# Reordering the sums of 512 slots on TensorE, and moving four weight loads on GpSimd's queue

## The chip, the core and the metric

The kernel runs on one core of one Trainium2 chip. The metric is the device time of one execution in microseconds. Before the change it is 2069.1 us, the median of three runs (2067.74 to 2071.44). Besides these runs there is one execution taken by the hardware profiler, and all rows below come from it.

## The reference, cut to what matters

Two transformer blocks over 256 tokens of width 1024, all in float32. The first block (recurrence, sparse attention, feed-forward) lies ahead of everything that the change touches. The second block has two layers; each ends in a layer of experts:

```python
s = einsum('thpe,pne->thpn', q, sub_keys)          # 8 heads, 2 halves, 128 keys
top_s, top_i = top_k(s, 16)
cand = top_s[:, :, 0, :, None] + top_s[:, :, 1, None, :]
best_s, best_j = top_k(cand, 16)                    # 16 experts a head of 16384
gate = softmax(best_s)
h = einsum('td,thkd->thk', x, u[expert])            # 128 experts a token
a = gelu(h) * gate
f = einsum('thk,thkd->td', a, v[expert])
```

Every token has experts of its own, so each row of `u` and `v` (1024 numbers each) has to be fetched from memory by index. The first layer mixes tokens by gated linear attention, the second by dilated attention with six heads of three groups. Both also attend to a memory of 256 tokens.

## The kernel before

Tokens lie on the 128 partitions, in two tiles. A pass is one layer of experts for one tile; there are four, in the order (layer 0, tile 0), (0, 1), (1, 0), (1, 1). A pass has 128 slots: slot s takes the s-th expert of each of its 128 tokens. All in all n runs from 0 to 511 (`SLOTS`). For each slot

- GpSimd issues one indirect DMA (L2254) that gathers 128 rows of u and v, 1 MB, into one of six buffers (`gbuf`, `GBUF = 6`); from n = 6 on it waits for `buffer_free` of slot n - 6, that is for the end of that slot's sum;
- VectorE multiplies the u half by x and adds up along the row, the dot (L2544), once the gather has landed;
- ScalarE takes the Gelu of the dot (L2082) and makes a diagonal matrix of gate x gelu (L2076, L2089; five buffers, `DIAGS`);
- TensorE multiplies that diagonal by the v half, two products of 512 columns that add into two PSUM banks over the whole pass (`add_slot`, L1456). That is the sum of the slot; it waits for `diag_ready`.

Beside the gathers of pass p, TensorE makes what is next: in pass 0 the queries and keys of the first layer of experts, in passes 1 and 2 the whole second layer for tiles 0 and 1: transposes, the products of dilated attention and of memory attention, the output product, the queries and keys of the experts; the last of these reach into the next pass. `pe_steps()` is a table written out by hand that says at which slot each of these products stands; `act_steps()` and `dve_steps()` say at which slot ScalarE and VectorE take their results, for most of them three slots later (`LATER = 3`). Each engine works through its table in order. ScalarE and VectorE do a slot's table entries before that slot's own diagonal or dot; VectorE's include the routing (top-k) of later experts and the soft-max of the scores. All of these products run through the helper at L925, so that rows of TensorE name L925 for them and L1456 for the sums. A product that streams its weights takes them from a ring of eight slots, filled in pairs of 1 MB by SyncE's queue (L1677).

The second layer's expert queries need 16 blocks of weights of 512 KB for each tile. The eight even ones (`KEPT`) are loaded once and kept in SBUF for both tiles, by `load_kept(i)` on GpSimd's queue. Blocks 0 to 3 have a place of their own and are loaded early. Blocks 4 to 7 go where the first layer's linear attention had its operands: 4 to 6 are loaded behind the wait for `gla_intra` (L2221), in front of the eighth row of gains and the weights of the first heads (`head_w`, L2231); 7 is loaded when the third sum of the linear attention is filled (`gla_o`, L2237). TensorE first waits for the kept blocks, all eight of them, at slot 224.

Of the kernel before, what the change touches and what calls it, by code (L numbers as in the profile page):

```python
# [17 lines left out]
P = 128  # L18
# [7 lines left out]
KEPT = tuple(range(0, 16, 2))  # L26
# [15 lines left out]
GBUF = 6  # L42
# [585 lines left out]
def build(nc, x_in, memT_in, weights, consts, where, rows_in, peer_uv, out):  # L628
# [5 lines left out]
    with ctx:  # L634
# [5 lines left out]
        def sem(name):  # L640

            if name not in named:
                named[name] = ctx.enter_context(nc.semaphore(name))
            return named[name]
# [190 lines left out]
        def wait_filled(e, key):  # L835

            e.wait_ge(sem("psum_filled"), ids[key] + 1)

        def wait_drained(e, key):

            n = ids[key]
            e.wait_ge(sem("drained_by_" + drains[n]), freed_count[n])

        def bank(key):
            return ps[banks[ids[key]]]
# [23 lines left out]
        def load_row(e, n):  # L869

            e.dma_start(rows[:, n % NROW, :], rows_in[n:n + 1, :].to_broadcast([P, D]))\  # L871
                .then_inc(sem(row_sem(n)), 16)
# [5 lines left out]
        def slot_of(q):  # L878

            return PASSES[q // P] + (q % P,)  # L880

        def wait_freed(e, q):

            e.wait_ge(sem(f"buffer_free{q % GBUF}"), q // GBUF + 1)
# [14 lines left out]
        def _(pe):  # L899
# [32 lines left out]
            def begin(key):  # L932

                b = before[ids[key]]
                if b is not None:
                    pe.wait_ge(sem("drained_by_" + drains[b]), freed_count[b])
                return bank(key)
# [512 lines left out]
            def add_slot(n):  # L1450

                pe.wait_ge(sem("diag_ready"), n + 1)
                for h in range(2):
                    key = (f"sum{n // P}", h)
                    b = begin(key) if n % P == 0 else bank(key)
                    ins = pe.matmul(b[:, :], diag[n % DIAGS], gbuf[n % GBUF][:, 1, h * 512:(h + 1) * 512],  # L1456
                                    start=n % P == 0, stop=n % P == P - 1)
                    if n == SLOTS - 1:
                        ins.then_inc(sem("psum_filled"), 1)
                    elif h == 1:  # L1460
                        ins.then_inc(sem(f"buffer_free{n % GBUF}"), 1)
                if n == SLOTS - P + CARRY:
                    pe.wait_ge(sem("alpha_ready"), 1)
                    for h in range(2):
                        pe.matmul(bank((f"sum{n // P}", h))[:, :], alpha_diag, x[:, NT - 1, h * 512:(h + 1) * 512],
                                  start=False, stop=False)
                if n % P == P - 1 and n < SLOTS - 1:

                    wait_freed(pe, n)
                    pe.sem_inc(sem("psum_filled"), 2)  # L1470
# [98 lines left out]
            def peer_keys(o, g):  # L1569

                wait_drained(pe, (f"peer_q1_{o}_{g}", 0))
                b = begin((f"peer_s1_{o}_{g}", 0))
                for hp in range(2 * TH):
                    mm(b[:, hp * P:(hp + 1) * P], tile_pq(g)[:, hp, :], c("keysT", 2, 2, PN)[:, 1, hp % 2, :],
                       True, True, end=hp == 2 * TH - 1)

            for n in range(SLOTS):
                for name, what in PE_STEPS.get(n, []):
                    if name == "second_turn":
                        pe.wait_ge(sem("x_ready"), 6)  # L1580
# [12 lines left out]
                    if name == "mem_k":  # L1593
                        i, half = what
# [5 lines left out]
                    if name == "mem_v" and n < P:  # L1600
                        i, half = what
# [17 lines left out]
                    if name == "dil_k":  # L1619
                        o, i = what  # L1620
# [5 lines left out]
                    if name == "qm":  # L1626
                        o, i = what
# [28 lines left out]
                    if name == "peer_q":  # L1656
                        o, g, i = what
# [5 lines left out]
                        block_of((f"peer_q1_{o}_{g}", 0), i, 4, tile_xT, kept=kept)  # L1663
                    if name == "peer_s":
                        peer_keys(*what)
                add_slot(n)

        @block.sync
        def _(sp):
# [517 lines left out]
        @block.gpsimd  # L2187
        def _(pool):

            pool.wait_ge(sem("psum_filled"), ids[("xT_mix", 3)] + 1)  # L2190
            pool.dma_start(cst[:, n_early:], consts[:, n_early:n_const]).then_inc(sem("consts_loaded"), 16)
            pool.wait_ge(sem("lru_scanned"), 1)
            pool.wait_ge(sem("gr_shaped"), 1)
            for j in range(NK):
                pool.tensor_tensor(xc[:, j, :], xc[:, j, :], gr[:, j, :], ALU.mult).then_inc(sem("pool_step"), 1)
            for j in range(NK + 1):
                if j < NK:
                    pool.wait_ge(sem("pool_step"), j + 1)
                    pool.wait_ge(sem("gmr_shaped"), j + 1)
                    pool.tensor_tensor(gmr[:, j, :], gmr[:, j, :], xc[:, j, :], ALU.mult).then_inc(sem("pool_step"), 1)  # L2200
                if j:
                    pool.wait_ge(sem("pool_step"), NK + j)
                    pool.tensor_tensor(xc[:, j - 1, :], xc[:, j - 1, :], gmr[:, j - 1, :], ALU.add)\
                        .then_inc(sem("recurrence_gated"), 1)
            pool.wait_ge(sem("psum_filled"), ids[("att_gate", 2 * len(GATES) - 1)] + 1)
            for n in range(NROW):
                load_row(pool, n)

            def load_kept(i):

                pool.dma_start(kept_queries[i], weights[n_slots - 8 + i // 2, :, i % 2 * SLOT:(i % 2 + 1) * SLOT])\
                    .then_inc(sem("kept_queries_loaded"), 16)

            for i in range(4):
                load_kept(i)
            pool.wait_ge(sem("psum_filled"), ids[("att_turn", 2 * len(UNITS) - 1)] + 1)
            pool.dma_start(memT[:, :, :], memT_in.rearrange("(k p) s -> p k s", p=P)).then_inc(sem("memT_loaded"), 16)
            pool.dma_start(spread, consts[:, n_const:]).then_inc(sem("spread_loaded"), 16)
            for r in range(NROW, SPREAD):
                if r == NROW + 3:  # L2220
                    wait_drained(pool, ("gla_intra", 0))  # L2221
                    pool.dma_start(kept_w, weights[n_slots - 2, :, :]).then_inc(sem("kept_loaded"), 16)
                    for i in range(4, len(KEPT) - 1):
                        load_kept(i)
                pool.wait_ge(sem("rows_used"), r - NROW + 1)
                load_row(pool, r)
                if r == 7:
                    wait_filled(pool, ("gla_r", 3))
                    wait_drained(pool, ("mem_value0", 2 * len(MEM_UNITS) - 2))
                    for i in range(4):  # L2230
                        pool.dma_start(head_w[i], weights[n_slots - 4 + i // 2, :, i % 2 * SLOT:(i % 2 + 1) * SLOT])\  # L2231
                            .then_inc(sem("head_loaded"), 16)
                    last = weights[n_slots - 1, :, :]
                    pool.dma_start(area(25168, 1024), last[:, 0:1024]).then_inc(sem("kept_out_loaded"), 16)
                    for i, m in enumerate((mem_k, mem_v)):
                        pool.dma_start(kept_out[1][i], last[:, 1024 + 512 * i:1536 + 512 * i]).then_inc(sem("kept_out_loaded"), 16)
            wait_filled(pool, ("gla_o", 3))  # L2237
            load_kept(len(KEPT) - 1)
            for n in range(SLOTS):
                l, t, s = slot_of(n)  # L2240
                if n == 0:
                    pool.wait_ge(sem("first_expert"), 1)
                elif n == 1:
                    pool.wait_ge(sem("next_experts"), 1)
                elif n == PK // 2:
                    pool.wait_ge(sem("peer_experts"), ROUTE_NO[0, 0, 0])
                elif (l, t, s) in ROUTE_NO:
                    pool.wait_ge(sem("peer_experts"), ROUTE_NO[l, t, s])
                if n == MIX_BUF:
                    wait_filled(pool, ("out0_1", 1))  # L2250
                if n >= GBUF:
                    wait_freed(pool, n - GBUF)
                pool.sem_inc(sem("gather_turn"), 1)
                pool.indirect_dma_start(gbuf[n % GBUF].rearrange("p a d -> p (a d)"), None, peer_uv,  # L2254
                                        bass.IndirectOffsetOnAxis(ap=expert[t][:, s:s + 1].bitcast(U32), axis=0))\
                    .then_inc(sem(f"gathered{n % GBUF}"), 16)
# [840 lines left out]
```

## Time and profile before

| | us |
|---|---|
| median of three runs | 2069.1 |
| profiled execution | 2072.7 |
| its span, first to last instruction | 2070.9 |
| TensorE busy with matmuls | 1895.9 |
| VectorE busy | 1382.5 |
| ScalarE busy | 896.6 |
| GpSimd busy | 616.1 |
| first gather issued at | 627.0 |

A page of the profile gives for each engine its busy time, and the span in 40 equal slices (51.8 us each) with the rate that the DMA engines moved. A row of the order of time has the start in us from the span's start, the duration, engine, line, operation, tiles, the number of records, and in brackets how long the engine was idle before it and what ended that. TensorE's matmuls are pipelined and their ends are modelled, so that the last record of a group reaches a little over the start of the next.

### The profile page before, as it was taken

The page shows a single profiled execution, that of the slowest core. Times are in us where ns is not written, and L with a number is a line of the kernel's source. Part 1 is how long each engine was busy: PE and PEld are TensorE (multiplying, and loading weights), DVE is VectorE, ACT ScalarE, POOL GpSimd, SP SyncE. Part 2 cuts the span into 40 slices and gives each one's busy share as a digit, 9 for nine tenths or more (in the row PEclk, how much of TensorE's full clock was granted, in tenths as well). Part 3 has the DMA queues.
Part 4 walks back from the last instruction along what each step waited for, and adds up shares of the span by engine and source line. Part 5 has one row for each costly group of instructions (what it writes and reads, how often), then busy time and mean ns, then how long its engine had stood idle before and what let it go on. Part 6 is the DMA issues. An engine that isn't in the chain of part 4 may idle for free. (4 is left out here: it accounts for less than half of the span.)

```text
span 2070.9 us, 24820 instructions
## 1 busy us (share of the span) xinstructions
PE 1895.9 (92%) x8012; PEld 1169.3 (56%) x8012; DVE 1382.5 (67%) x2957; ACT 896.6 (43%) x2417; POOL 616.1 (30%) x567
## 2 busy tenths in 40 slices
PE   8999999999998999988899998999999899877776
PEld 8788668887955654433456544556664355322222
DVE  8778666666738677776665545766865575985444
ACT  5657454444534333333334533343455334343332
POOL 0002200000003344444333334443334434444442
PEclk9999999999999999999999999999999999999999
DMA  6623555554658999999999999999999999999997
GB/s 253 224 108 123 194 184 192 193 183 152 235 186 354 390 421 419 418 418 414 400 421 421 421 419 410 417 422 421 417 414 391 416 416 387 422 421 419 421 419 317
DMA packets 99373, 708.06 MB, mean 342 GB/s; under 512 B 11040, under 2 KB 11184, under 8 KB 14896
## 3 DMA queue, kind: packets, MB, share of 16 engines
q0 software_dynamic: 77504, 552.25, 65.1%
q1 hardware_dynamic: 21600, 154.15, 19.8%
q8 instruction: 64, 1.05, 0.2%
q14 instruction: 61, 0.50, 0.1%
q10 hardware_dynamic: 144, 0.11, 0.0%
HBM read 705.42 MB, written 1.05 MB: 341 GB/s over the span
## 5 line engine op out<-in xcount | busy, mean ns | idle before, releaser
L1456 PE MATMUL bank<-arena 128*128 128x512 f32 x2048 | 980.6, 609 | 145.4 <-ACT arena L2089 142.1
L2544 DVE SCALAR_TENSOR_TENSOR arena<-arena,x_tok 128x1024 f32<-128x1024 f32 x512 | 627.1, 1226 | 466.7 <-DMA arena<-peer_uv,arena 461.1
L2254 POOL DMA_INDIRECT arena<-peer_uv,arena x512 | 580.9, 1135 | 850.1 <-PE bank L1456 649.4
L1456 PEld LDWEIGHTS bank<-arena 128*128 128x128 f32 x2048 | 362.0, 191 | 639.4 <-ACT arena L2089 339.7
L2082 ACT ACTIVATE arena<-arena 128x1 f32<-128x1 f32 x512 | 103.6, 202 | 841.7 <-DVE arena L2544 837.7
L2089 ACT ACTIVATE arena<-arena 128x128 f32<-128x128 f32 x512 | 197.7, 386 | 0.5
L2076 ACT ACTIVATE arena<-const_tile,arena 128x128 f32<-128x128 f32 x512 | 197.8, 386 | 0.0
L925 PEld LDWEIGHTS bank<-xT,weight_ring 128*128 128x128 f32 x1248 | 165.5, 191 | 37.0 <-issue 31.1
L925 PE MATMUL bank<-xT,weight_ring 128*128 128x128 f32 (+1 forms) x1248 | 177.2, 294 | 0.9 <-DVE xT L2281 0.9
L925 PE MATMUL bank<-x_low_high,z_high 128*128 128x512 f32 (+1 forms) x480 | 135.8, 351 | 1.5 <-issue 1.5
L1201 PE MATMUL bank<-x_split,w_split 128*128 128x512 f32 x704 | 129.0, 342 | 2.6 <-DVE x_split L2824 2.6
L1201 PEld LDWEIGHTS bank<-x_split,w_split 128*128 128x128 f32 x704 | 110.4, 190 | 20.0 <-issue 2.8
L2806 DVE TENSOR_TENSOR w_split<-weight_ring,w_split 128x1024 fp32r<-128x1024 f32 x66 | 80.8, 1225 | 36.9 <-ACT w_split L1917 36.2
L925 PE MATMUL bank<-x_low_high,ring_low 128*128 128x256 f32 x368 | 104.0, 283 | 0.0
L925 PEld LDWEIGHTS bank<-x_low_high,z_high 128*128 128x128 f32 x480 | 83.5, 190 | 17.1 <-issue 5.2
L871 POOL DMA_DIRECT2D row_ring<-rows_in x8 | 4.5, 571 | 286.6 <-DVEq L2354 200.4
L1917 ACT ACTIVATE w_split<-weight_ring 128x1024 fp32r<-128x1024 f32 x66 | 69.7, 1060 | 42.7 <-PE bank L1201 26.6
L1704 ACT ACTIVATE arena<-bank 128x512 f32<-128x512 f32 (+6 forms) x143 | 67.7, 498 | 45.0 <-PE bank L925 38.1
L925 PE MATMUL bank<-arena 128*64 128x128 f32 (+10 forms) x664 | 74.7, 311 | 2.5 <-DVE arena L2304 1.8
L925 PEld LDWEIGHTS bank<-x_low_high,ring_low 128*128 128x128 f32 x368 | 70.5, 192 | 0.0
L925 PEld LDWEIGHTS bank<-arena 64*128 64x128 f32 (+6 forms) x664 | 54.4, 169 | 28.1 <-issue 23.6
L1767 ACT ACTIVATE z_high<-weight_ring 128x1024 fp32r<-128x1024 f32 x50 | 51.8, 1053 | 34.3 <-PE bank L925 25.5
(322 smaller groups left out, 2035.7 us busy)
## 6 DMA issues: line engine op xcount, KB each, us to landing
weight_ring<-weights SPq DMA_DIRECT2D x145, 1024.0 KB
arena<-peer_uv,arena POOLq DMA_INDIRECT x512
arena<-weights POOLq DMA_DIRECT2D x9, 512.0 KB, 7.9
row_ring<-rows_in POOLq DMA_DIRECT2D x8, 512.0 KB, 4.7
kept_queries<-weights POOLq DMA_DIRECT2D x4, 512.0 KB, 9.8
const_tile<-consts POOLq DMA_DIRECT2D x1, 1657.0 KB, 8.9
x_tok<-x_in SPq DMA_DIRECT2D x2, 512.0 KB, 4.9
memT<-memT_in POOLq DMA_DIRECT2D x1, 1024.0 KB, 7.5
```

Of the source, the lines that this page charges most:

```text
L925: ins = pe.matmul(o, lhsT, rhs, start=start, stop=stop, is_transpose=turn or None)
L1201: ins = pe.matmul(o, lhsT, rhs, start=start, stop=stop)
L1456: ins = pe.matmul(b[:, :], diag[n % DIAGS], gbuf[n % GBUF][:, 1, h * 512:(h + 1) * 512], start=n % P == 0, stop=n % P == P - 1)
L1704: done(act.activation(o, i, f, **kw), "drained_by_act" if last else "act_step")
L1767: done(act.activation(z_high[:, i % SPLITS, :], ring[:, slot % RING, :], ACT.Copy, scale=scale), "z_high")
L1917: done(act.activation(w_split[n % SPLITS][:, 0, :], ring[:, slot % RING, :], ACT.Copy), "slot_high")
L2076: done(act.activation(gate_diag[n % 2], ident, ACT.Copy, scale=w[:, s:s + 1]), "gate_diag")
L2082: done(act.activation(hdot[:, s:s + 1], hdot[:, s:s + 1], ACT.Gelu), "peer_gelu")
L2089: done(act.activation(diag[n % DIAGS], gate_diag[n % 2], ACT.Copy, scale=hdot[:, s:s + 1]), "diag_ready")
L2254: pool.indirect_dma_start(gbuf[n % GBUF].rearrange("p a d -> p (a d)"), None, peer_uv, bass.IndirectOffsetOnAxis(ap=expert[t][:, s:s + 1]. ...
L2544: dve.scalar_tensor_tensor(u, u, 1.0, x[:, t, :], ALU.mult, ALU.mult, accum_out=hdot[:, s:s + 1])\
L2806: done(dve.tensor_tensor(w[:, 1, :], ring[:, slot % RING, :], w[:, 0, :], ALU.subtract), name)
```

## The change

Two things. First, in the loop over the slots on TensorE, the sum of slot n is put ahead of the other products of slot n in place of behind them. This holds from slot 12 (two rounds of the six buffers) on, and not for the first and the last slot of a pass. Second, on GpSimd's queue the loads of kept blocks 4 to 6 stand behind the loads of the first heads' weights and of the output weights, and block 7 is loaded at slot 64 of the first pass, between the wait for the buffer and the gather of that slot. The wait for `gla_o` is dropped.

```diff
@@ -1575,6 +1575,9 @@
             for n in range(SLOTS):
+                ahead = 0 < n % P < P - 1 and n >= 2 * GBUF
+                if ahead:
+                    add_slot(n)
                 for name, what in PE_STEPS.get(n, []):
...
@@ -1663,7 +1666,8 @@
                     if name == "peer_s":
                         peer_keys(*what)
-                add_slot(n)
+                if not ahead:
+                    add_slot(n)
...
@@ -2220,8 +2224,6 @@
                     pool.dma_start(kept_w, weights[n_slots - 2, :, :]).then_inc(sem("kept_loaded"), 16)
-                    for i in range(4, len(KEPT) - 1):
-                        load_kept(i)
                 pool.wait_ge(sem("rows_used"), r - NROW + 1)
...
@@ -2234,8 +2236,8 @@
-            wait_filled(pool, ("gla_o", 3))
-            load_kept(len(KEPT) - 1)
+            for i in range(4, min(len(KEPT), 7)):
+                load_kept(i)
             for n in range(SLOTS):
...
@@ -2250,6 +2252,8 @@
                 if n >= GBUF:
                     wait_freed(pool, n - GBUF)
+                if n == 2 * P // 4 and len(KEPT) == 8:
+                    load_kept(7)
                 pool.sem_inc(sem("gather_turn"), 1)
```

## Rows read from the trace of the kernel before

**Rows 1.** The page: the span, and the DMA rate in 40 slices.

```profile
span 2070.9 us, 24820 instructions
...
GB/s 253 224 108 123 194 184 192 193 183 152 235 186 354 390 421 419 418 418 414 400 421 421 421 419 410 417 422 421 417 414 391 416 416 387 422 421 419 421 419 317
```

**Rows 2.** Waits, whole span: who waited for whom, us, times, longest.

```profile
POOL arena L2254 <- PE bank L1456: 649.4, 347, 9.2
...
DVE arena L2544 <- DMA arena<-peer_uv,arena: 461.1, 376, 3.7
```

**Rows 3.** Order of time, a slot with nothing but its gather and sum.

```profile
1906.87 1.98 PE L1456 MATMUL bank<-arena 128*128 128x512 f32 x4 [0.50 <-ACT arena L2089]
...
1907.24 1.23 DVE L2544 SCALAR_TENSOR_TENSOR arena<-arena,x_tok 128x1024 f32<-128x1024 f32 x1 [1.25 <-DMA arena<-peer_uv,arena]
...
1908.91 0.39 ACT L2089 ACTIVATE arena<-arena 128x128 f32<-128x128 f32 x1
...
1909.35 1.12 PE L1456 MATMUL bank<-arena 128*128 128x512 f32 x2 [0.50 <-ACT arena L2089]
...
1909.98 1.79 POOL L2254 DMA_INDIRECT arena<-peer_uv,arena  x1 [1.86 <-issue]
```

**Rows 4.** Busy time by stretch: PE, PEld, DVE, ACT, POOL, granted clock, DMA share, GB/s.

```profile
1560.00:1580.00 20.00, 18.63 (x79) 10.90 (x78) 12.09 (x25) 13.56 (x34) 8.80 (x7) 1.00 0.98 378
...
1700.00:1720.00 20.00, 20.00 (x97) 12.93 (x97) 15.01 (x30) 10.84 (x31) 7.26 (x7) 1.00 0.98 373
```

**Rows 5.** Order of time, TensorE and ScalarE, slots 293 to 295.

```profile
1482.45 3.70 PE L1456 MATMUL bank<-arena 128*128 128x512 f32 x8 [0.93 <-ACT arena L2089]
...
1485.72 0.39 ACT L2089 ACTIVATE arena<-arena 128x128 f32<-128x128 f32 x1
...
1489.07 1.88 PE L1456 MATMUL bank<-arena 128*128 128x512 f32 x4
```

**Rows 6.** Order of time, TensorE and ScalarE, slots 370 to 373.

```profile
1704.78 1.95 PE L925 MATMUL bank<-const_tile,arena 128*128 128x128 f32 x16
...
1706.16 0.39 ACT L2089 ACTIVATE arena<-arena 128x128 f32<-128x128 f32 x1
...
1706.60 1.98 PE L1456 MATMUL bank<-arena 128*128 128x512 f32 x4
...
1710.20 1.88 PE L1456 MATMUL bank<-arena 128*128 128x512 f32 x4
...
1712.81 3.60 PE L1456 MATMUL bank<-arena 128*128 128x512 f32 x8
```

**Rows 7.** Order of time, gather 378 on GpSimd and its dot.

```profile
1715.51 0.94 POOL L2254 DMA_INDIRECT arena<-peer_uv,arena  x1 [1.67 <-PE bank L1456]
...
1723.24 1.22 DVE L2544 SCALAR_TENSOR_TENSOR arena<-arena,x_tok 128x1024 f32<-128x1024 f32 x1 [1.25 <-DMA arena<-peer_uv,arena]
```

**Rows 8.** Order of time: waits for products at slots 64 and 318.

```profile
820.90 0.38 ACT L1704 ACTIVATE arena<-bank 128x256 f32<-128x256 f32 x1 [2.98 <-PE bank L925]
...
1551.86 1.88 PE L1456 MATMUL bank<-arena 128*128 128x512 f32 x4
...
1556.09 3.70 PE L1456 MATMUL bank<-arena 128*128 128x512 f32 x8
...
1556.19 0.76 DVE L2585 COPY arena<-bank 128x256 f32<-128x256 f32 x2 [3.02 <-PE bank L925]
```

**Rows 9.** Order of time on GpSimd: kept loads and the first gather.

```profile
560.07 1.57 POOL L2211 DMA_DIRECT2D arena<-weights  x3
...
619.22 0.54 POOL L2211 DMA_DIRECT2D arena<-weights  x1 [24.52 <-PE bank L925]
626.98 1.02 POOL L2254 DMA_INDIRECT arena<-peer_uv,arena  x1 [7.22 <-DVE arena L2474]
```

**Rows 10.** Busy time by stretch, ahead of the gathers (columns as in Rows 4).

```profile
570.00:580.00 10.00, 9.26 (x65) 7.59 (x64) 8.72 (x18) 5.50 (x15) 0.00 (x0) 1.00 0.57 222
...
600.00:610.00 10.00, 10.00 (x24) 4.18 (x22) 3.14 (x6) 0.29 (x1) 0.00 (x0) 1.00 0.26 105
```

## The prediction

> **What bounds the kernel now.** I read the page first, then the waits, then the DMA rate by stretch, then the order of time in the stretches where that rate falls. From 673 us to the end the DMA engines move about 421 GB/s in most of the page's slices [rows 1]: 512 gathers of 1 MB, one a slot, and the weights between them. In the waits VectorE stands for the landing of gathers and GpSimd for TensorE, whose sum of slot n frees the buffer of gather n + 6 [rows 2]. Where a slot carries nothing else, sums come 2.48 us apart (1906.87 and 1909.35): a dot starts at the landing (1907.24), its diagonal ends at 1909.30, the sum starts at 1909.35, and the gather that a sum lets go is issued 1.1 us behind that sum's end (1908.85, then 1909.98) [rows 3]. So the stage goes at the pace of its DMA bytes. A sum that ends earlier pays only where the DMA has too few gathers before it.
>
> How much that is can be read off one row. The page's slices are 51.8 us wide; each slice's shortfall is (421 - x) / 421 x 51.8 us. From the slice at 673 us on these add up to about 21 us [rows 1]. Slice 390 (3.8 us) is the start of the loop, and its hole lies at 672 to 688 us, before sum 12 can free a buffer. Slice 400 (2.6 us) and slice 410 (1.3 us) lie where a layer norm holds the dots and so the diagonals. What TensorE's order can touch is the slice 391 (3.7 us, 1553 to 1605), 387 (4.2 us, 1708 to 1760), and small ones (two of 414, two of 416 and others, about 5 us together). Inside the two large ones TensorE is busy 18.63 and 20.00 of 20 us and the rate is 378 and 373 GB/s at a DMA share of 0.98 [rows 4]: packets last longer there, they hardly stop.
>
> **Part 1, the order on TensorE.** Call A(n) the sum of slot n (four records, 1.72 us), and W(n) that slot's other products: 16 records, 1.78 us, for a block of 128 columns; 8 records, 0.89 us. Nothing is added or taken away. Before, A(n) can start at the later of its diagonal and the end of W(n); after, at the later of its diagonal and the end of W(n - 1), which stands behind A(n - 1). Two things follow. Where TensorE waits for data at every slot, nothing changes. Where it is behind, A(n) moves by W(n0) - W(n), with n0 the last slot at which it still waited: a block that used to fill the wait for the diagonal of n0 now comes behind A(n0) and is paid in full. So the change can go either way, stretch by stretch. I worked it through the four stretches below; the slots are counted by the sums, four records each (a ninth record or a missing one shows up as x9 or x7).
>
> Gain (slots 295 to 303). TensorE waited 0.93 us before the sum of slot 293, with no product there; sums 293 and 294 follow each other from 1482.45 to 1485.9, and A(295) starts at 1489.07, behind 3.1 us of products, though its diagonal was there at 1486.11 (1485.72 + 0.39) [rows 5]. So W(n0) = 0: sums 295 and 296 come 2.9 us earlier, 297 1.6 us, and so gathers 301 to 303. The slices there are short by 0.4 and 0.9 us, and that is all that can be won. With the other small shortfalls I take -1.5 us for all of these, bounds -3.0 and 0.
>
> Loss (slots 370 to 389). W(370) runs from 1704.78 and ends just as the diagonal of 370 gets ready (1706.16 + 0.39): it was hidden [rows 6]. W(371) lies between 1708.3 and 1710.20, W(372) between 1711.9 and 1712.81. After the change A(370) still starts at 1706.6, then come W(370) to 1710.1, A(371) to 1711.8 (before: 1710.20 to 1711.92, no change), W(371) to 1713.6, and A(372) at 1713.6 in place of 1712.81; W(372) is 0.89, so A(373) starts at 1716.2 in place of 1714.5, and A(374) at 1717.9 (before 1718.03). From there a sum without products of its own (375, 377, 378, 380, 382, and on to 389) is 1.6 to 1.7 us later, and one with a block is where it was. Eleven gathers go out later, in just the stretch in which the DMA is short of them: gather 378 is issued at 1715.51 and its dot starts at 1723.24, 7.7 us later [rows 7], where the full rate goes with 9 to 10 us. Each microsecond of lateness is lost once, as all later landings then shift. Bounds: 0, and 3.4 us (twice the shift, since the rate is low too); I take +1.5.
>
> The scores (slots 309 to 326). VectorE waited 3.02 us at 1556.19 for the products of memory attention that end W(315) (L2585), with the dot of slot 318, whose data had landed, queued behind [rows 8]. A(314) started at 1551.86 and A(315) at 1556.09, so W(315) is 2.5 us; W(313) and W(314) are like W(295), 3.1 each. W(309) holds scores too, and 1.7 us more on them puts the diagonal and sum of slot 313 at about 1546.4. From there three sums and three sets, 3 x 1.72 + 3.1 + 3.1 + 2.5 = 13.9, end these scores at 1560.3 in place of 1556.1, so the dot, ScalarE's diagonal, the sums 317 to 320 and gathers 323 to 326 are 1.5 to 2.7 us late. Against that, gathers 319 and 320 go out up to 3 us earlier. Bounds -2.0 (half of the slice's shortfall won) and +3.5; I take +1.2. The same products stand in pass 1 (slots 184 to 203), with no shortfall now but with sums 188 to 190 up to 2.5 us later: bounds 0 and 1.8, I take +0.8. At slot 64 ScalarE waited 2.98 us for W(63) ahead of that slot's diagonal [rows 8]; W(63) now ends 2.2 us later, and sums 64 to 66 with it, while 62 and 63 come 1.3 us earlier: bounds -0.4 and +1.8, I take +0.2.
>
> **Part 2, the loads of the kept slots.** Three loads of 512 KB leave the POOL queue at 560.07, and follow the loads that end at 594.7 (24.52 us of idle before 619.22) [rows 9]. What they left: TensorE was busy 9.26 of 10 us at 570 to 580, so at most 0.7 us could be won; its one gap there ended with a ScalarE drain that began as the transposes ended, so I take 0. What they enter: 1.5 MB at 421 GB/s is 3.7 us, in 600 to 610, where the DMA moves 105 GB/s at a share of 0.26 [rows 10]; they stand behind the head weights in their queue, so these don't wait. The cover is that empty stretch; without it they would cost 3.7 us. The wait for the third sum of the linear attention goes too, but GpSimd's first gather at 626.98 stood for VectorE's index (7.22 us) anyway: 0. The last load moves from 619.22, where it cost nothing, to slot 64, in front of gather 64: 0.5 MB at 421 GB/s is 1.2 us of the resource that sets the pace, plus 0.54 us of issue on GpSimd, hidden as gathers go out some 10 us ahead of their dots there. Bounds 0 (it falls into a hole made by ScalarE's wait) and 1.2; I take +1.2.
>
> The Trainium skill speaks to this move. DMA: Bandwidth & Descriptors, Rules for kernel authors, says to issue a DMA early and wait for it late; by that rule the load should have stayed at 619, and the sum would be 1.2 us less. Its section Issuing engines are not separate DMA queues says that all DMAs share the same 16 engines, so that a load from another queue would cost the same here. The trace can't show the moved load, but the even 421 GB/s of [rows 1] has no room for it.
>
> **The sum.** +1.2 (load) - 1.5 (heavy slots and small holes) + 1.2 (slice 391) + 1.5 (slice 387) + 0.8 (pass 1) + 0.2 (slot 64) + 0 (front) = +3.4 us. The profiled execution took 2072.7 us (span 2070.9 and 1.8 around it) and would take 2076.1; the runs' median is 2069.1, so I forecast 2072.5 us. All lower bounds together give 2063, all upper ones 2081.
>
> **The rivals.** (1) The order helps as a buffer freed early: the holes of slices 391 and 387 don't deepen, the heavy slots win their 3.0 and the scores 2.0, slot 64 0.4; with the load's 1.2 that is -4.2, 2064.9 us. For it: TensorE is behind its diagonals by 3 us at slot 295 [rows 5]. Against it: the hidden blocks. (2) Clearly slower: the scores behind two sums hold the dots. It decides from the point at which a score ends later than its dot's data lands, in both passes. Price: 3.5 in place of 1.2 and 1.8 in place of 0.8, so +3.4 + 3.3 = +6.7, 2075.8 us. For it: the wait of 3.02 us is there already [rows 8]. Against it: in pass 1 VectorE doesn't wait at all. (3) The reordering does nothing, as the DMA sets the pace and a gather early or late by 2 us is absorbed by the queue; only the load counts: 2070.3 us. A rule of the skill stands for (3): Perfetto Trace Analysis, Identifying the Most-Contended Engine, has one improve the engine with the highest occupancy first, and that is the DMA here.
>
> **How the numbers follow.** The forecast holds 0.35, (1) 0.20, (2) 0.25, (3) 0.20. A measurement of this kernel can tell about 0.2% from no change, that is 4.1 us: under 2065.0 is faster, over 2073.2 slower. (1) lies on the edge, and with the low tail of (3) gives 0.15 for faster; (2) and near a third of the forecast's spread give 0.35 for slower; 0.50 stays for within. The range from 2064.5 to 2078.0 holds the forecast, (3), most of (2) and half of (1).
>
> **What would show it.** In the profile after: the load of 512 KB at slot 64, near 808 us, and a DMA rate not under 420 there; slice 387 lower than 387; VectorE's wait at L2585 near 1556 longer than 3.02 us; the slice at 1501 up from 414; nothing changed before 627 us and after 1770 us but a shift. The forecast is wrong if slices 391 and 387 rise towards 421, or if TensorE's start moves ahead of 627.

## The result, and where the time went

The changed kernel takes 2079.9 us (median of five runs, 2079.0 to 2087.4) beside 2069.1 for the kernel before: a ratio of 1.0053, with a 95% interval from 1.0036 to 1.0069. The medians differ by 10.8 us, where 3.4 were forecast. The forecast of 2072.5 and its range up to 2078.0 were both too low.

The profiled execution of the changed kernel, the page's span and DMA rate in 40 slices (these answer to [rows 1]):

```profile
span 2078.1 us, 24821 instructions
...
GB/s 237 223 137 108 203 196 192 190 162 182 203 183 386 400 418 415 421 416 417 409 421 416 398 413 414 415 422 421 421 394 372 410 418 373 420 422 421 421 421 317
```

A slice is 52.0 us now. Four slices are low that weren't, or weren't as much: 398 (1143 to 1195 us, pass 1), 394 and 372 (1507 to 1611, pass 2; 414 and 391 before), and 373 (1714 to 1766; 387 before). The first gather goes out at 623.27, 3.7 us earlier than at 626.98 [rows 9]. That is not the change: in the twelve kernels below it goes out between 620 and 627, whichever place the loads have. So I count from there. From the first gather to the end of the span it was 1443.9 us before and is 1454.8 after: 10.9 us, as much as the medians differ by.

The surest way to see where they lie is the landing of the gathers (a gather lands where its last packet comes in, and where VectorE waits for it its dot starts there, as in [rows 3]). The time between two landings, in us:

| gathers | before | after | order alone | loads alone | scores ahead | copies later | memory scores ahead |
|---|---|---|---|---|---|---|---|
| 0 to 60 | 175.7 | 176.5 | 176.8 | 176.1 | 175.9 | 176.1 | 175.8 |
| 60 to 130 | 181.7 | 182.7 | 181.8 | 183.0 | 182.7 | 183.5 | 182.9 |
| 130 to 175 | 142.1 | 141.3 | 141.0 | 141.5 | 141.0 | 141.0 | 141.1 |
| 175 to 205 | 84.7 | 89.1 | 89.7 | 84.8 | 85.4 | 85.6 | 86.2 |
| 205 to 290 | 251.3 | 250.3 | 253.6 | 251.3 | 253.3 | 251.2 | 250.8 |
| 290 to 306 | 50.4 | 48.5 | 47.7 | 50.4 | 47.9 | 49.4 | 48.7 |
| 306 to 345 | 116.8 | 124.1 | 123.0 | 116.9 | 117.3 | 118.3 | 118.2 |
| 345 to 395 | 134.0 | 135.1 | 137.6 | 136.2 | 136.1 | 136.9 | 137.5 |
| 395 to 511 | 290.5 | 290.6 | 291.8 | 290.2 | 290.7 | 290.9 | 291.6 |

Each column is one profiled execution; kernels that don't differ in a stretch lie up to 1 to 3.5 us apart there (gathers 205 to 290 take 250.3 to 253.6 us in the five kernels with the new order). The columns from "order alone" on belong to experiments that are told below. Of the 10.9 us, +7.3 lie between gathers 306 and 345 and +4.4 between 175 and 205, the two places where memory scores are taken. Slots 290 to 306 won 1.9. All else adds up to +1.1.

Who waited for whom in the changed kernel, from 661 to 2066 us (us in total, times, longest; [rows 2] is over the whole span):

```profile
POOL arena L2258 <- PE bank L1456: 655.8, 345, 4.9
DVE arena L2548 <- DMA arena<-peer_uv,arena: 436.3, 360, 3.7
...
ACT arena L1708 <- PE bank L925: 31.8, 18, 5.3
DVE arena L2589 <- PE bank L925: 19.1, 4, 6.8
DVE arena L2571 <- PE bank L925: 6.4, 3, 2.7
DVE xT L2605 <- PE bank L925: 6.0, 6, 2.7
```

Lines stand 3 or 4 lower than before: L2589 is VectorE's copy of the memory scores (L2585 before), L2571 that of the dilated scores, L2605 that of the attention values. Before, L2585 waited 4.1 us in two waits (1.12 at 1536.62, and the 3.02 of [rows 8]) and the other two not at all. ScalarE's waits for products (L1708) grew as well, from 10.9 us in four waits over the same stretch to 31.8 in eighteen; the experiments below show that they are not what costs the time. Order of time on VectorE in pass 2 (answers to the last row of [rows 8]):

```profile
1538.12 0.76 DVE L2589 COPY arena<-bank 128x256 f32<-128x256 f32 x2 [4.63 <-PE bank L925]
...
1550.82 1.02 DVE L2571 SCALAR_TENSOR_TENSOR arena<-bank,const_tile 128x512 f32<-128x512 f32 x2 [2.70 <-PE bank L925]
...
1562.01 0.76 DVE L2589 COPY arena<-bank 128x256 f32<-128x256 f32 x2 [6.76 <-PE bank L925]
...
1563.52 1.23 DVE L2548 SCALAR_TENSOR_TENSOR arena<-arena,x_tok 128x1024 f32<-128x1024 f32 x1
```

The dot at 1563.52 is that of slot 318, whose data had landed at 1554.24: 9.3 us behind its data (3.3 before). What TensorE did meanwhile:

```profile
1535.51 1.95 PE L925 MATMUL bank<-xT,weight_ring 128*128 128x128 f32 x16
1537.39 0.70 PE L925 MATMUL bank<-mem_k,arena 64*128 64x256 f32 x4
1538.02 5.71 PE L1456 MATMUL bank<-arena 128*128 128x512 f32 x12
1543.56 0.61 PE L925 MATMUL bank<-arena,memT 128*128 128x128 f32 x4
1546.24 3.65 PE L1456 MATMUL bank<-arena 128*128 128x512 f32 x4 [2.07 <-ACT arena L2093]
1549.68 1.54 PE L925 MATMUL bank<-arena 128*128 128x256 f32 x6
...
1561.28 0.70 PE L925 MATMUL bank<-mem_k,arena 64*128 64x256 f32 x4
```

The rows of 64x256 are the memory scores of slots 309 and 315. Between them TensorE ran out of work for 2.07 us: behind the wait of 4.63 us the dot of slot 313 started at 1541.30, 1.9 us after its data had landed, ScalarE did an exponential before its diagonal (ready at 1546.19), and the blocks that could have filled the wait (L925 at 1549.68 and on) now stand behind that sum. Then the sum itself took 3.65 us for four records in place of 1.88. The stretches (columns as in [rows 4]) say why:

```profile
1544.00:1546.00 2.00, 0.17 (x2) 0.00 (x0) 1.86 (x6) 1.97 (x5) 1.22 (x1) 1.00 1.00 418
1546.00:1550.00 4.00, 3.76 (x6) 1.67 (x7) 1.37 (x3) 1.70 (x7) 0.00 (x0) 0.57 1.01 418
1550.00:1554.00 4.00, 4.00 (x25) 3.28 (x24) 3.11 (x4) 0.00 (x0) 0.94 (x1) 1.00 0.89 311
1554.00:1558.00 4.00, 4.00 (x31) 3.51 (x30) 1.25 (x4) 2.66 (x6) 0.94 (x1) 1.00 0.64 209
```

The granted clock is 0.57 from 1546 to 1550, that is at its lower level (1.2 GHz) for nearly all of the sum, right behind the 2.07 us of idling. And the last two rows show the price: the DMA falls to 311 and 209 GB/s, and its share to 0.64. Over 50 us, first in the kernel before, then in the changed kernel, the rate went from 389 to 343 GB/s and the DMA's share from 0.99 to 0.93:

```profile
1550.00:1600.00 50.00, 47.14 (x190) 26.17 (x189) 28.38 (x55) 26.97 (x74) 21.78 (x19) 1.00 0.99 389
1550.00:1600.00 50.00, 46.24 (x208) 27.97 (x207) 27.33 (x51) 24.91 (x65) 17.82 (x17) 1.00 0.93 343
```

GpSimd issues the gathers 319 to 322 into this hole:

```profile
1550.70 0.94 POOL L2258 DMA_INDIRECT arena<-peer_uv,arena  x1 [4.94 <-PE bank L1456]
1555.52 0.94 POOL L2258 DMA_INDIRECT arena<-peer_uv,arena  x1 [3.89 <-issue]
1560.69 0.94 POOL L2258 DMA_INDIRECT arena<-peer_uv,arena  x1 [4.24 <-issue]
1564.72 0.95 POOL L2258 DMA_INDIRECT arena<-peer_uv,arena  x1 [3.09 <-PE bank L1456]
```

They stand 4 to 5 us apart, where a landing every 2.48 us needs one every 2.48 us. Before, 319 to 321 stood as far apart (1549.71, 1554.86, 1558.89), but 322 followed after 1.7 us, at 1560.60. And one more thing differs: a weight load of 1 MB on SyncE's queue, first in the kernel before, then in the changed kernel.

```profile
1550.64 0.33 SPq L1677 DMA_DIRECT2D weight_ring<-weights  x1
1556.46 0.33 SPq L1681 DMA_DIRECT2D weight_ring<-weights  x1
```

Before, its bytes moved at 1552 to 1558 us, just where only about two gathers were under way, and the rate from 1554 to 1558 us was 395 GB/s. In the changed kernel it goes out 5.8 us later, and its bytes move from 1560 us on, behind the hole. So in these traces late gathers and a late weight load make the hole together; what each is worth alone was not measured. Counted from the landing of gather 306 (1518.4 before, 1517.1 after), gather 320 goes out 2.0 us later than before, 321 3.2, and 322 to 328 between 4.6 and 7.2.

### The profile page after: what moved, and what is told of

It is laid out like the page before. It is cut to its first block and busy times, and to the rows that moved or that the text cites. A ratio compares the mean times of both kernels' runs of the same rounds, so it can differ in the third digit from the quotient of the medians.

```text
span 2078.1 us, 24821 instructions
## 1 busy us (share of the span) xinstructions
PE 1893.3 (91%) x8012; PEld 1166.7 (56%) x8012; DVE 1383.0 (67%) x2957; ACT 897.8 (43%) x2417; POOL 615.1 (30%) x567
## 5 line engine op out<-in xcount | busy, mean ns | idle before, releaser
L925 PEld LDWEIGHTS bank<-xT,weight_ring 128*128 128x128 f32 x1248 | 167.2, 193 | 37.7 <-issue 30.9
L925 PE MATMUL bank<-xT,weight_ring 128*128 128x128 f32 (+1 forms) x1248 | 179.5, 296 | 0.8 <-DVE xT L2285 0.8
L925 PE MATMUL bank<-x_low_high,z_high 128*128 128x512 f32 (+1 forms) x480 | 136.0, 351 | 0.0
L925 PE MATMUL bank<-x_low_high,ring_low 128*128 128x256 f32 x368 | 104.2, 283 | 0.0
L1708 ACT ACTIVATE arena<-bank 128x512 f32<-128x512 f32 (+6 forms) x143 | 68.1, 500 | 71.6 <-PE bank L925 63.4
L925 PEld LDWEIGHTS bank<-x_low_high,z_high 128*128 128x128 f32 x480 | 83.7, 190 | 15.0 <-issue 2.9
L925 PE MATMUL bank<-arena 128*64 128x128 f32 (+10 forms) x664 | 72.9, 305 | 1.8 <-DVE arena L2308 1.0
L925 PEld LDWEIGHTS bank<-x_low_high,ring_low 128*128 128x128 f32 x368 | 70.8, 192 | 0.0
L925 PEld LDWEIGHTS bank<-arena 64*128 64x128 f32 (+6 forms) x664 | 52.7, 161 | 27.8 <-issue 24.0
L925 PE MATMUL bank<-weight_ring,arena 128*128 128x512 f32 (+1 forms) x192 | 64.9, 528 | 0.2 <-ACT arena L1708 0.2
```

What stands on the lines that cost most here:

```text
L925: ins = pe.matmul(o, lhsT, rhs, start=start, stop=stop, is_transpose=turn or None)
L1708: done(act.activation(o, i, f, **kw), "drained_by_act" if last else "act_step")
```

## The experiments

The theory, T: a product that VectorE waits for ends later, the dots behind it in VectorE's queue start late, so diagonals, sums and buffers are late, and the DMA runs out of gathers. Its rivals: S, that the sums are late by themselves, since blocks that used to fill a wait for a diagonal are now paid in full, whoever waits for the scores; and L, that the load in the loop does more than move its bytes. Ratios are against runs of the kernel before on the same chip. Its median was 2069.9 us for the two parts, for scores ahead and for copies later; 2072.0 for scores behind, the gain, the hidden blocks and the first attempt on the old kernel; and 2070.6 for the rest. The ratios on record are not quite those of the medians (up to 0.08% away). Their interval, given in brackets, is a 95% one; 0.1% is 2.1 us.

**The two parts, each alone.** The order alone is the first two hunks of the diff, the loads alone the other three.

> The kernel before with the new order of TensorE alone; the loads of the kept blocks stay where they were. Theory (T): what the change costs is VectorE and ScalarE waiting for products that now end up to two sums later, with dots queued behind them, so that gathers go out late and the DMA runs short; the load of block 7 is a term of its own, 0.5 MB at 421 GB/s = 1.2 us. In the two profiled executions the stage of the gathers is 10.9 us longer, so T gives +9.7 us against the kernel before, about 2079, and the DMA's shortfall at 1174 to 1200 us and 1550 to 1600 us as in the changed kernel. Rival (L): the load at slot 64 sets off more than its bytes (it takes the place of a gather in the queue, and later slots stay behind): then at most +5 us, under 2074.

> The changed kernel with the old order on TensorE: only the loads are moved. T: +1.2 us against the kernel before (bounds 0 and 1.2), about 2070.3, and a DMA rate of 421 GB/s around slot 64 with no hole beside it. L: +5 us or more. If the two ends don't add up (this and the run with the order alone, against 10.8 us for both), the two parts act on each other.

Order alone: 1.0052 (1.0035 to 1.0069), 2081.3 us. Loads alone: 1.0010 (0.9998 to 1.0022), 2073.3 us. So the order carries the loss, and L's "under 2074" for the order alone is out. VectorE's wait with the order alone is the changed kernel's, almost to the tenth (the idling at 1544 and the clock behind it are there again, 2.08 us and 0.59):

```profile
DVE arena L2589 <- PE bank L925: 19.3, 4, 6.8
```

The load itself stands between two gathers (GpSimd, changed kernel):

```profile
805.16 0.57 POOL L2215 DMA_DIRECT2D arena<-weights  x1 [1.42 <-PE bank L1456]
806.04 1.34 POOL L2258 DMA_INDIRECT arena<-peer_uv,arena  x1 [0.30 <-issue]
```

With it gathers 60 to 130 take 183.0 us in the loads alone (182.7 to 183.5 in the other kernels with that load); seven kernels of this study with the old order there and without it take 181.2 to 181.8.

**Scores ahead of the sum.** Each list of PE_STEPS is sorted so that scores stand first, and then

```diff
+                scores = [step for step in PE_STEPS.get(n, []) if step[0] in ("dil_score", "mem_score")]
-                if ahead:
+                if ahead and not scores:
                     add_slot(n)
-                for name, what in PE_STEPS.get(n, []):
+                for i, (name, what) in enumerate(PE_STEPS.get(n, [])):
+                    if ahead and scores and i == len(scores):
+                        add_slot(n)
...
-                if not ahead:
+                if not ahead or scores and len(scores) == len(PE_STEPS[n]):
                     add_slot(n)
```

> The changed kernel, but in a slot that holds scores (of dilated or of memory attention: eight slots in each of passes 1 and 2) the order on TensorE is scores, sum, the slot's other products, in place of sum, other products, scores. So scores end 1.7 us (the sum) and, where a block stands in the slot, a further 0.9 to 1.8 us earlier. T: VectorE's waits of 2.9 to 6.8 us at its copies of the memory scores (L2589 of the changed kernel) fall under 3 us, most of the 9.7 us comes back: 2070 to 2074. Rival (S): the sums themselves are late, since blocks that used to fill the wait for a diagonal now stand behind the sum and are paid in full; who waits for the scores doesn't matter. S gives no gain: 2078 to 2081.

1.0011 (1.0001 to 1.0020): the loss falls from 0.53% to 0.11%, which is what the loads alone cost (0.10%). VectorE never waited over 1.1 us for memory scores, and both stretches are back (85.4 and 117.3 us in the table). All other sums stand where they do in the changed kernel, and 2.4 us are still won in slots 290 to 306. So S is out as the cause of the loss. ScalarE's waits for products are still there (32.6 us in eighteen), so it isn't they that cost the time either.

**VectorE's copies a slot later.** Here TensorE's program is the changed kernel's, instruction for instruction; only the consumer moves.

```diff
-            add(steps, b + 33 + APART * u + LATER, "dil_soft", o, u)
+            add(steps, b + 34 + APART * u + LATER, "dil_soft", o, u)
...
-            add(steps, b + 53 + APART * m + LATER, "mem_soft", o, m)
+            add(steps, b + 54 + APART * m + LATER, "mem_soft", o, m)
```

> The changed kernel with TensorE's order untouched; VectorE takes the scores of both attentions out of their banks one slot later (four slots behind the product in place of three). ScalarE's exponentials stay where they are, so that they now wait for VectorE. T: the same products are waited for a slot (about 2.5 us) later, VectorE's wait at L2589 falls from 19.1 us in four waits to under 10, and 4 to 8 us come back: 2072 to 2076. S: the sums are late for TensorE's own work, which is unchanged here: 2079 to 2081.

1.0006 (0.9994 to 1.0019), 2072.0 us, at the low end of T's forecast. The waits at L2589, and ScalarE's for products:

```profile
DVE arena L2589 <- PE bank L925: 3.0, 3, 1.8
ACT arena L1708 <- PE bank L925: 38.3, 24, 5.3
```

This is the clearest test of T: the products stand where they stood, VectorE waits 3.0 us for the memory scores in place of 19.1, and over 9 us come back, though ScalarE waits longer than in the changed kernel.

**The converse: scores behind the sum in the old order.** The kernel before, where in the slots with scores TensorE does the other products, the sum, and then the scores.

```diff
+                others = [step for step in PE_STEPS.get(n, []) if step not in scores]
+                if scores and not others:
+                    add_slot(n)
+                for i, (name, what) in enumerate(others + scores):
+                    if scores and i and i == len(others):
+                        add_slot(n)
...
-                add_slot(n)
+                if not scores:
+                    add_slot(n)
```

> The kernel before, loads and order as they were, but in the eight slots of passes 1 and 2 that hold scores these scores stand behind the sum of the slot in place of ahead of it; in such a slot the other products come first. No other sum moves. Theory (T): holding a score back by one sum (1.7 us) is enough to hold the dots: VectorE's waits at the memory scores grow from 4.1 us in two waits to over 10, slots 306 to 345 take 3 to 7 us longer between landings than before (116.8 us), slots 175 to 205 1 to 4 us longer (84.7); in all 2074 to 2079. Rival (S): only the place of the sums counts; they move ahead of the scores here, so 2068 to 2070.

1.0003 (0.9992 to 1.0014): a miss. The waits did grow as forecast,

```profile
DVE arena L2592 <- PE bank L925: 10.2, 4, 5.0
DVE arena L2574 <- PE bank L925: 3.8, 4, 1.5
```

and its profile has 119.9 us between gathers 306 and 345 (+3.1) and 85.8 between 175 and 205 (+1.1), the low ends of what I gave; but over all runs it can't be told from the kernel before. (The profiled execution was the slowest of the twelve, 2078.4 us.) So one sum's delay isn't enough for the loss: at the upper end of the interval it is worth 2.9 us. TensorE's gap at this place was 0.58 us here, before 1547.34, with the clock at full speed behind it; a block that stands ahead of the sum filled the rest. The full loss needs both: late scores, and the new order around them. Late scores alone cost at most 2.9 us (this run), the new order with early scores next to nothing (1.0011 with the load in it). That the link is TensorE's gap is read from the traces and wasn't tested by itself.

**Which scores.** The changed kernel with the memory scores alone ahead of the sum.

```diff
+                scores = [step for step in PE_STEPS.get(n, []) if step[0] == "mem_score"]
```

> The changed kernel, with the scores of memory attention alone (slots 181, 187, 309, 315) ahead of the sum of their slot; those of dilated attention stay behind it. Theory (M): VectorE waits 19.1 us in four waits for the memory scores and 6.4 us in three for the dilated ones, and two of these three stand behind a first wait for memory scores: so nearly all of the gain of moving both (from 2080 to 2073) is here: 2072 to 2075. Rival: the dilated scores hold as much: 2076 to 2078.

1.0014 (1.0005 to 1.0023), 2073.3 us: moving four slots' products gives back all but 0.6 of the 8.7 us that moving all sixteen slots' gave; with intervals of some 2 us either way the two can't be told apart.

**The gain and the hidden blocks, each alone**: the order in 17 slots of passes 1 and 2, and in 352 to 395.

```diff
+                ahead = n // P in (1, 2) and 34 <= n % P <= 50
...
+                ahead = 352 <= n < 396 and 0 < n % P < P - 1
```

> The kernel before, with the new order only at 17 slots of passes 1 and 2 (162 to 178 and 290 to 306), ahead of the memory scores. T: this is the gaining term of the prediction by itself. Between the landings of gathers 290 and 306 the changed kernel needed 48.5 us, the kernel before 50.4: here 47.7 to 48.9, with at most 1 us given back behind slot 306; in all -1 to -2 us, 2067.5 to 2069. Rival: the gain is given back in full in slots 306 to 345, since TensorE has the same work before the memory scores: 2069 to 2071.

> The kernel before, with the new order only at slots 352 to 395 (not at 383 and 384). T: a block of the expert queries that used to fill the wait for the diagonal now stands behind the sum and is paid in full: slots 367 to 395 take 1.2 to 2.0 us longer than before (75.1 us between landings), all else as before: 2071 to 2072. Rival: nothing, or up to 3.4 us, the ends of the prediction's bounds.

The first: 0.9989 (0.9979 to 1.0000), 2.3 us less, at the edge of what can be told. Gathers 290 to 306 take 49.3 us, just under the 49.5 to 51.3 of six kernels with the old order there and the copies in their old place, and 0.6 is given back in 306 to 345, as VectorE waits longer there (7.2 us in three waits for memory scores). The second: 0.9992 (0.9983 to 1.0002), so the loss that I forecast for hidden blocks doesn't show in the time. In its trace gathers 367 to 395 take 77.1 us, as in the changed kernel; but eight kernels with the old order there take 75.1 to 76.5, of which the kernel before is the lowest, and all six with the new one 76.3 to 78.1. The means are 1.0 us apart; the time of this run allows 0.4 us at most. So this term is 0 to 1 us.

**Bytes in the loop.** The kernel before with all four loads, one each at slots 64 to 67.

```diff
+                if 64 <= n < 68:
+                    load_kept(n - 60)
```

> The kernel before with its order, but all four loads of the kept blocks 4 to 7 (0.5 MB each) stand in the loop, one each at slots 64 to 67, in place of one there as in the change. Theory (B): a load in the loop costs its bytes, 0.5 MB at 421 GB/s = 1.24 us, so four cost 5.0 us and the stretch from the landing of gather 60 to that of gather 130 goes from 181.7 us to 186.7 (one load alone: 182.9 in the run with the loads moved); in all +5 us, about 2075 beside 2070. Rival: the queue takes them in its slack, +0 to +2.

1.0030 (1.0018 to 1.0043), 6.2 us (3.7 to 8.9); gathers 60 to 130 take 185.5 us, 4.0 more than the 181.5 of the kernels without. Loads in the loop cost about their bytes (1.0 to 1.5 us each), and aren't absorbed.

**Can the old kernel gain by this?** Three attempts: memory scores ahead of the block of their slot; copies a slot later; both, with the order of the 17 slots.

```diff
+    for listed in steps.values():
+        listed.sort(key=lambda step: step[0] not in ("dil_score", "mem_score"))
```

That is the first; the second has the edit of the copies shown above, and the third has both and `ahead = n // P in (1, 2) and 34 <= n % P <= 50`.

> The kernel before, with one move: at the two slots of each pass that hold memory scores (181, 187, 309, 315) the scores stand ahead of the block of the dilated queries of the same slot in place of behind it. T: the 3.02 us that VectorE waits at 1556.19 for them falls by the block, 1.8 us, and slots 306 to 345 take 0.5 to 1.8 us less than 116.8 us: 2068 to 2069.5. Rival: the dot behind the wait costs nothing today, no change.

> The kernel before with VectorE's copies of the scores one slot later (four slots behind the product), nothing else. If a wait for scores with dots queued behind it costs time in the kernel before too (1.12 us at 1536.62 and 3.02 us at 1556.19), slots 306 to 345 take 1 to 3 us less than 116.8 us: -1 to -2 us. Rival: ScalarE's exponential, which stays, then waits for VectorE and holds the diagonal instead: 0 to +2 us.

> The kernel before with three parts: the new order at slots 34 to 50 of passes 1 and 2 only, the memory scores ahead of the block in their slot, and VectorE's copies of the scores one slot later. The loads stay. If the parts add up (1 us in slots 290 to 306, 1 to 2 us in slots 306 to 345), this is 2 to 4 us under the kernel before; if the stage is bound by its DMA bytes but for some 21 us of shortfall that have other causes, not more than 1 us.

0.9991 (0.9979 to 1.0003), 0.9998 (0.9989 to 1.0007) and 0.9995 (0.9983 to 1.0007). The waits go: 0.84 us is the only one for memory scores in the first (3.02 before), there is none in the other two, and gathers 306 to 345 take 116.6, 115.4 and 116.3 us against 116.8. That is up to 1.4 us of a stretch, against run-to-run differences of several us in the whole. None is shown to be faster than the kernel before, and all of them are better than the changed kernel.

## Why the prediction was wrong, step by step

- **What bounds the kernel**: right. The stage goes by its DMA bytes and loses where the gathers are late; the page's slices located the loss.
- **Gain in slots 290 to 303, -1.5 us**: right. -1.9 in the changed kernel, -2.7 with the order alone, -1.1 by itself (where the old order varies by 1.8 from kernel to kernel, with the kernel before in its middle).
- **The scores, slots 309 to 326, +1.2 us (bounds -2.0 and +3.5)**: this is the term that failed: +7.3, and +6.1 with the order alone. Its first half held: sum 313 was put at 1546.4 and started at 1546.24. The scores were put at 1560.3 and were there at 1562.01; the 1.7 us between are the sum that ran at a granted clock of 0.57 behind 2.07 us of idling, which I had taken at full speed. (These are times from the start of the span. The changed kernel lands gather 306 1.4 us earlier than the kernel before; counted from there, as the gathers are counted here, the sum is 1.2 us later than I put it and the scores 3.1.) The second half is what failed, the step from the late scores to "1.5 to 2.7 us late" for sums 317 to 320 and gathers 323 to 326: gathers 323 to 326 are 4.6 to 5.9 us late. I followed one wait, the last one. The trace has three in a row (4.63, 2.70, 6.76 us), and behind each wait for memory scores stands ScalarE, which does their exponentials ahead of the next diagonal (as it did before, at 1559.77; I had left it out of the chain):

```profile
1565.59 1.28 ACT L1739 ACT_TABLE_LOAD   x1
...
1569.29 0.20 ACT L2086 ACTIVATE arena<-arena 128x1 f32<-128x1 f32 x1
...
1569.69 0.39 ACT L2093 ACTIVATE arena<-arena 128x128 f32<-128x128 f32 x1
```

  The dot of slot 319 was at 1565.19, its diagonal is made at 1569.69. The cover that I counted on was the gathers 319 and 320 going out "up to 3 us earlier"; they went out 2.4 and 2.0 us later. And the forecast has no term for the weight load that went out 5.8 us later. In short: I priced one late score by one sum, where the trace shows a feedback through dot, diagonal, an idle TensorE and the next score.
- **Pass 1, +0.8 us (bounds 0 and 1.8)**: the same failure, +4.4 (+3.4 over the mean of the four kernels that leave this stretch as it was, 84.7 to 87.5). That VectorE doesn't wait at all there before was taken for slack; the slack was less than the delay of one sum and one wait. Now it waits 2.86 and 4.81 us.
- **Hidden blocks, slots 370 to 389, +1.5 us**: +2.0 between the two profiles, about +1 against all kernels with the old order, and nothing that the time of that part alone shows. Too high rather than too low, inside its bounds (0 to 1 us, see above).
- **The load, +1.2 us**: right; +1.3 in its stretch; four loads cost 4.0 us in theirs (1.0 each) and 6.2 in the whole. **Front, 0**: right; the kept loads run in the empty stretch that ends before 605 us, and the first gather waits for VectorE as before. **Slot 64, +0.2 us**: right, 181.8 against 181.7 us with the order alone.
- **The rivals**: (2) was what happened, in both passes and from the point that it named. Its price, 6.7 us, was summed from the two upper bounds that were themselves too low. (1) had its gains, 1.9 us of them, and they were buried. (3) was wrong for the order, right for the loads.
- **The rule of the Trainium skill** that DMAs are to be issued early (DMA: Bandwidth & Descriptors, Rules for kernel authors) points the way the runs went: the load that went from an idle stretch into the loop costs its bytes, +1.3 us in its stretch. The page's reason, a fixed setup cost that overlaps, is another, and no run here shows it.
- **What would show it**: L2585's wait near 1556 did grow beyond 3.02 us, slice 387 did fall (373), the load is there at 805 us. "Slices 391 and 387 rise towards 421" did not come. Two signs failed. The slice at 1501 was to go up from 414; the one that starts at 1507 now has 394, as the hole at 1550 reaches into it. And the rate near 808 us was to stay at 420; it is 403 GB/s from 800 to 810.

Summed: -1.9 + 7.3 + 4.4 + 1.0 (gathers 60 to 130, the load in it) + 1.1 (345 to 395) and -1.0 elsewhere is 10.9 us.

## What to carry to other kernels

When a producer is moved behind something else, look at who waits for it in order, and what is queued behind the waiter, before counting the producer's own engine; price the whole feedback (late dot, late diagonal, an idle producer, the next late score), not one wait. An engine that doesn't wait at all may be a fraction of one operation from waiting, so measure the slack (when the data is ready against when it is wanted) in place of reading a zero as safety. And work that fills a wait should stand ahead of it, where somebody is short of time; only what others wait for comes first of all. The runs show the second half of this last sentence; for the first they have the gap of 2.07 us with blocks queued behind the sum, and 0 to 1 us in the slots of the hidden blocks.

## What the runs showed of the hardware that I had not expected

- TensorE's granted clock falls to its lower level for short stretches in the middle of the stage, in the kernel before as well. There it did so at 997, 1260 and 1464 us, behind idling of 2.04, 2.00 and 1.97 us; in the changed kernel at 1089 and 1546 us, behind 2.06 and 2.07 us (0.57 from 1546 to 1550 us, 0.59 over the same stretch with the order alone). It doesn't always do so: with the scores ahead TensorE was idle for 2.32 us before 1481.26, and the eight records behind that took 3.70 us, full speed. It is no general cost of the new order: over the stage the clock stood at its lower level for about 14 us in the kernel before and about 7 in the changed one, by the same rows. It hurt where it fell between two scores that others waited for.
- How much the DMA moves goes with how many gathers are under way, and with whether a weight load stands beside them. Counted in steps of 1 us from 680 to 2050 us, where no weights moved: with four gathers under way 419 GB/s on average in both kernels, with three 403 (before) and 397 (after), with two 368 and 339. With one under way as the next is issued and no weights beside it (1554 to 1558 us in the changed kernel) it was 209 GB/s; with about two and the weight load beside them (the same stretch before) it was 395. In the hole a gather took 5.6 to 7.7 us from issue to landing, where half of all gathers take 9.4 to 11 us: each was faster, all together slower.
